# A hybrid SSD, attention and PEER block on one core: the attention's query chunks in pairs over three engines

## The reference, cut to what matters

```python
xn = rmsnorm(h, norm1_g)
z, xbc, dt_raw, q, k, v = split(xn @ w_in)
xbc = silu(causal_depthwise_conv(xbc, conv_w, conv_b))
dt = softplus(dt_raw + dt_bias)
y_ssd = rmsnorm_by_group(ssd_scan(xs, bs, cs, dt, a_log, d_skip) * silu(z), ssd_norm_g)
y_att = rmsnorm(swa_sink_attention(q, k, v, sinks), attn_norm_g)
h = h + concatenate([y_ssd, y_att]) @ w_out
h = h + peer_ffn(rmsnorm(h, norm2_g), wq, keys, u_tab, v_tab)
return rmsnorm(h, norm_f_g)
```

## Time and profile before

| | |
|---|---|
| median of 3 runs | 1706.69 us (1706.01 to 1706.77) |
| the profiled execution | 1707.13 us |
| its span, first to last instruction | 1705.4 us |
| mean granted TensorE clock | 0.998 |
| busy share of the span | PE 99%, DVE 79%, ACT 55%, POOL 33% |

### The profile page before, as it was taken

How to read it: one execution, slowest core, us unless ns; L and a number is a source line. 1 busy time by engine, 2 the same in 40 slices (tenths; PEclk the granted TensorE clock), 3 DMA queues, 4 the chain that set the end, 5 groups by cost and what they waited for, 6 DMA issues and landing times.

```text
span 1705.4 us, 26529 instructions
## 1 busy us (share of the span) xinstructions
PE 1693.4 (99%) x9481; PEld 1472.6 (86%) x9481; DVE 1343.7 (79%) x2129; ACT 930.9 (55%) x1605; POOL 569.1 (33%) x358
## 2 busy tenths in 40 slices
PE   9999999999999999999999999999999999999997
PEld 8889998988888888888888888888888888888886
DVE  7998888878999998554554666668888888888887
ACT  7556755544455554554454454455555555555556
POOL 0120000000017788777783000058555422222210
PEclk9999999999999999999999999999999999999999
DMA  7665568786668887777787888899999999999995
GB/s 272 199 225 172 178 213 267 237 235 199 206 195 197 196 193 197 194 192 201 194 191 221 261 264 262 268 357 340 375 344 361 356 365 365 358 365 365 359 334 157
DMA packets 187042, 444.70 MB, mean 261 GB/s; under 512 B 59472, under 2 KB 94560, under 8 KB 178400
## 3 DMA queue, kind: packets, MB, share of 16 engines
q1 hardware_dynamic: 146688, 371.89, 65.1%
q0 software_dynamic: 40000, 71.55, 15.7%
q10 hardware_dynamic: 288, 0.53, 0.1%
HBM read 423.27 MB, written 20.05 MB: 260 GB/s over the span
## 4 chain that ended last, share of the span: by engine, by line
PE 94%; DVE 3%; ACT 1%; DMA 1%; issue 0%; POOL 0%; SPq 0%; DVEq 0%; ACTq 0%
PE ps L1984 23%; PE ps L2430 20%; PE ps L1990 12%; PE ps L1970 7%; PE ps L2419 7%; PE ps L2421 7%; PE ps L1968 4%; PE ps L2000 3%; PE ps L2319 2%; PE ps L2003 2%; PE ps L2235 1%; PE ps L2322 1%; PE ps L2236 1%; PE ps L2237 1%; DVE low L1088 1%; DMA raw<-v_tab 1%
## 5 line engine op out<-in xcount | busy, mean ns | idle before, releaser
L1088 DVE TENSOR_TENSOR low<-raw,high 128x1024 fp32r<-128x1024 f32 x376 | 458.2, 1224 | 66.3 <-ACT high L705 56.5
L705 ACT ACTIVATE high<-raw 128x1024 fp32r<-128x1024 f32 x376 | 393.1, 1051 | 38.5 <-PE ps L2003 18.9
L1984 PE MATMUL ps<-acts,high 128*128 128x512 f32 x1472 | 350.5, 390 | 0.0
L1984 PEld LDWEIGHTS ps<-acts,high 128*128 128x128 f32 x1472 | 272.7, 188 | 54.1
L656 POOL DMA_INDIRECT big<-v_tab,half_sb x64 | 121.0, 1890 | 465.0 <-DVE big L1856 278.1
L698 ACT ACTIVATE high<-raw 128x1024 fp32r<-128x1024 f32 x172 | 182.6, 1062 | 164.5 <-PE ps L2430 162.4
L1095 DVE TENSOR_TENSOR low<-raw,high 128x1024 fp32r<-128x1024 f32 x172 | 206.2, 1223 | 58.4 <-ACT high L698 58.0
L636 POOL DMA_INDIRECT gate_scratch<-gates_sb,cells_sb x128 | 215.3, 1682 | 69.8 <-issue 69.8
L982 ACT ACTIVATE side<-ps 128x256 f32<-128x256 f32 x128 | 49.1, 383 | 316.2 <-PE ps L1990 213.3
L1990 PEld LDWEIGHTS ps<-acts,low 128*128 128x128 f32 x1472 | 188.8, 191 | 7.2
L1990 PE MATMUL ps<-acts,low 128*128 128x256 f32 x1472 | 191.0, 283 | 0.0
(11 more groups left out here) (311 smaller groups left out, 2925.1 us busy)
## 6 DMA issues: line engine op xcount, KB each, us to landing
raw<-u_tab SPq DMA_DIRECT2D x256, 512.0 KB, 4.4
raw<-v_tab SPq DMA_DIRECT2D x172, 512.0 KB, 7.3
raw_more<-v_tab SPq DMA_DIRECT2D x84, 512.0 KB, 7.5
raw<-w_in SPq DMA_DIRECT2D x60, 512.0 KB, 4.7
raw<-w_out SPq DMA_DIRECT2D x32, 512.0 KB, 5.1
raw<-w_q SPq DMA_DIRECT2D x32, 512.0 KB, 5.2
gate_scratch<-side SPq DMA_DIRECT2D x32, 384.0 KB, 5.7
big<-gate_scratch SPq DMA_DIRECT2D x16, 768.0 KB, 7.1
```

The lines of the kernel that those rows point to most:

```text
L705: nc.scalar.activation(slot(high, s), slot(raw, s), ACT.Copy).then_inc(hi_done, 1)
L1088: V.tensor_tensor(slot(low, s), slot(raw, s), slot(high, s).bitcast(F32), ALU.subtract).then_inc(lo_done, 1)
L1984: mm(both, tile_of(high, kk), both_of(kk), start=(kk == 0), stop=False, skip_group_check=True)
```

## The change

Four edits.

1. `IN_SPLIT` grows by chunks 2 and 3 and by the eight query chunks. So chunks 2 and 3 and all query chunks are projected in pairs (`product_pairs`, `half_pairs`), ACT copies, DVE adds instead of `take`, POOL multiplies.
2. The exponential of the time steps moves from the end of the step c = 5 on ACT, ahead of the first silu, into the step c = 6, ahead of the first tap.
3. `out_pairs` does all sixteen 512-wide matmuls of a chunk and then all sixteen 256-wide ones, instead of eight and eight for each half of the inputs. It waits for `high` first and for `low` later, and both halves' `used` come at the end of their 256-wide matmuls.
4. POOL's list gets the additional multiplies: chunks 2 and 3 first, the query chunks after z.

```diff
-IN_SPLIT = (4, 5, 6, 7, 8, 9) + tuple(range(C_Z, C_Z + SSD_TILES))
+IN_SPLIT = tuple(range(2, 10)) + tuple(range(C_Z, C_Q + SSD_TILES))
...
+            if c >= C_Q:
+                return view(QZ + (c - C_Q) * T, T)
...
-            for c in range(4, 10):
+            for c in range(2, 10):
                 normalise(c)
...
-            for c in range(C_Z + 4, C_Q):
+            for c in range(C_Z + 4, C_OUT):
                 normalise(c)
...
+            copy_low(2)
             for c in range(4, C_Z):
                 cut_high_piece(c + 1, (c + 1) % 2, 0)
+                if c == 6:
+                    act.wait_ge(dt_neg, 1)
+                    nc.scalar.activation(dtv[2], dtv[1], ACT.Exp).then_inc(dt_exp, 1)
                 for k in convs(c):
                     first_tap(k)
                 if c - 1 in IN_SPLIT:
                     copy_low(c - 1)
                 cut_high_piece(c + 1, (c + 1) % 2, 1)
-                if c == 5:
-                    act.wait_ge(dt_neg, 1)
-                    nc.scalar.activation(dtv[2], dtv[1], ACT.Exp).then_inc(dt_exp, 1)
                 for k in convs(c - 1):
                     silu(k)
...
                 if s:
                     exps(s - 1)
+                copy_low(c - 1)
...
-                take(c - 1, (c - 1) % 2, view(QZ + s * T, T), rstd1)
+                add_low(c - 1)
...
-            product(2, 0)
-            product(3, 1)
+            product_pairs(2)
+            product_pairs(3)
...
-            product(C_Q, C_Q % 2)
+            product_pairs(C_Q)
...
-                part(c, 0, every, acc, normed, True, False).then_inc(used, 1)
+                half_pairs(c, 0, True, False).then_inc(used, 1)
...
-                part(c, 1, every, acc, normed, False, True).then_inc(used, 1)
+                half_pairs(c, 1, False, True).then_inc(used, 1)
...
-                for half in range(2):
-                    pe.wait_ge(lo_done, 2 * c + half + 1)
-                    part_pairs(c, half, pair_bank(m) + half).then_inc(used, 1)
+                bank, at = pair_bank(m), 2 * (c % 2) * PIECE
+                for kk in range(KT):
+                    if kk % 8 == 0:
+                        pe.wait_ge(hi_done, 2 * c + kk // 8 + 1)
+                    wh = high[:, at + kk * P:at + (kk + 1) * P]
+                    mm(ps[:, bank + kk // 8, :], wh, act2_both(kk), start=kk % 8 == 0, stop=False, skip_group_check=True)
+                for kk in range(KT):
+                    if kk % 8 == 0:
+                        pe.wait_ge(lo_done, 2 * c + kk // 8 + 1)
+                    wl = low[:, at + kk * P:at + (kk + 1) * P]
+                    ins = mm(ps[:, bank + kk // 8, 0:T], wl, plain(act2_hi)(kk), start=False, stop=kk % 8 == 7,
+                             skip_group_check=True)
+                    if kk % 8 == 7:
+                        ins.then_inc(used, 1)
```

More of the change, by code:

```diff
@@ L2253, in spread @@
                 ins.then_inc(rows_ok, 1)
-            product(C_Q, C_Q % 2)
+            product_pairs(C_Q)
             pe.wait_ge(y_out, SSD_HEADS)
-            normed, mixed = (hi_tile, lo_tile), (plain(act2_hi), plain(act2_lo))
+            mixed = (plain(act2_hi), plain(act2_lo))
             every = range(8)
@@ L2260, in _ @@
                 c = C_Q + 1 + s
-                acc = ps[:, c % 2, 0:T]
                 pe.wait_ge(taken, c - 1)
                 pe.wait_ge(lo_done, 2 * c + 1)
-                part(c, 0, every, acc, normed, True, False).then_inc(used, 1)
+                half_pairs(c, 0, True, False).then_inc(used, 1)
                 if s:
@@ L2312, in _ @@
             part(c1, 1, range(7, 8), att_acc[1], mixed, False, True).then_inc(used, 2)
-            def part_pairs(c, half, bank):
-                s = 2 * (c % 2) + half
-                for k in range(8):
-                    wh = high[:, s * PIECE + k * P:s * PIECE + (k + 1) * P]
-                    mm(ps[:, bank, :], wh, act2_both(8 * half + k), start=(k == 0), stop=False, skip_group_check=True)
-                for k in range(8):
-                    wl = low[:, s * PIECE + k * P:s * PIECE + (k + 1) * P]
-                    ins = mm(ps[:, bank, 0:T], wl, plain(act2_hi)(8 * half + k), start=False, stop=(k == 7),
-                             skip_group_check=True)
-                return ins
             def out_pairs(m):
```

## The result

The changed kernel takes **1712.19 us** (median of 8 runs, 1711.29 to 1713.06), beside 1706.34 for the kernel before on the same chip (8 runs, 1706.01 to 1707.06): ratio 1.0033, 95% interval 1.0024 to 1.0042. The medians are 5.85 us apart, the changed kernel the slower. The profiled execution took 1712.57 us with a span of 1710.9; before, the span was 1705.4.

What follows compares the result with a forecast made beforehand. TensorE's back-to-back matmuls (94% of the span) bound the kernel; early +0.35, attention +6.1 and output -0.2 gave +6.2 us, so 1712.9 us. Forecast case 1708.5 to 1715.5 (chance 0.62), overall range 1705.5 to 1716.5.

Steps and rivals of the forecast that it cites:

- Bound and method: Whole kernel: TensorE's matmuls, 94% of the span, bound it; time taken off PE or spent waiting counts in full.
- The attention, +6.1: Attention's eight logits steps: POOL's multiply waits for DVE's cut (1.65 us), logits come late, PE waits; +6.1 us.
- Rival A: Attention: POOL isn't held up, its multiply takes 0.75 us; +0.3 us in all, 1707.0 us; chance 0.18.
- B: Attention and early part: PE never waits, all pairing is kept; -2.6 us, 1704.1 us; chance 0.07.
- C: Attention steps 1, 6, 7 and chunk 5: POOL passed over again by a second two-input DVE instruction; +4.3, 1717; chance 0.13.
- The early part, +0.35 forecast: Chunks 2 to 8: POOL's multiplies delay DVE 0.8 us before chunk 6, the moved exponential saves 0.44; about +0.35 us.
- the 0.44: Chunk 7: PE's second early wait, about 0.44 us, removed by moving the exponential one chunk later.
- D: Chunks 5 and 6: two added table loads delay ACT's copies, early part stays late; 0.4 us, no separate chance.
- The output, -0.2: Ten output chunks: ordering matmuls by width saves 0.02 us each, 0.2 us in all.

Runs made afterwards that it cites:

- cut_later: Against the changed kernel: in the attention, DVE's cut behind the add, and the low parts of y, made behind the maxes; 1714.28 us, ratio 1.0046.
- dve_waits: Against the changed kernel: in attention steps other than the third, DVE waits for POOL's multiplied query pair before its next cut; 1710.58 us, ratio 1.0024.
- warm_pool: Against the changed kernel: one extra POOL multiply of zeros ahead of its first useful one; 1711.84 us, ratio 1.0030.

## Why the prediction was right, point by point

**Bound and method.** Right: PE's matmuls stay the chain, and each microsecond of waiting in front of them came out as time. Forecast 1712.9, measured 1712.19; against the kernel before, 6.2 us were forecast and 5.85 measured.

**The attention, +6.1.** Right in mechanism and size. POOL's multiply: 1.65 forecast, 1.63 to 1.64 measured. Late steps: 8.80 and 8.79. Gaps forecast 8.27, 8.49, 8.27, 4 times 8.80; measured 8.26, 8.53, 8.32, 8.80, 8.79, 8.79, 8.79. C grew by 6.14: the first logits come 0.51 us late behind chunk 8 (0.5 forecast), the eight take 6.05 us more (6.0), and the rest is 0.42 shorter (0.4). PE's idle time, said to be some 1.4 us in front of each late logits, is 0.43, 1.30, 1.31 and 0.85. Three independent edits (a wait, a halved cut, another engine for the multiply) each moved it as the theory says. The transposes behind the last logits came 6.69 us on (6.70 forecast).

**Rival A.** It did not come: POOL was held up. Its price for the late steps, 7.9 us, was met where POOL was free of the cut (7.88, twice, in cut_later). Its sum, +0.95 for the attention, was not tested, since no run has POOL free with DVE's order and times left alone: dve_waits makes DVE stand still for 0.84 us a step (+4.3 with 0.73 us multiplies), and cut_later moves the cut, which fits elsewhere only in some of the steps. The Trainium skill, GPSIMD Engine Reference, section 3.1, gave 0.82 us by its ratio; the traces show 0.72 to 0.75 for a multiply with no DVE instruction of two SBUF inputs beside it, and 1.64 with the cut.

**Rivals B and C.** B, no waits, did not come. C, passed over again, did not come in the attention: in the last two steps a second instruction of two SBUF inputs stands behind the first, and there it was DVE that waited for POOL (1.75 us instead of 1.22; in step 1, at 164.72, 1.22 instead of 0.68):

```profile
206.82 1.21 DVE L1092 TENSOR_TENSOR low<-raw,high 128x1024 fp32r<-128x1024 f32 x1
207.95 1.75 DVE L1496 TENSOR_TENSOR act_all<-big,act_all 128x1024 fp32r<-128x1024 f32 x1
```

**The early part, +0.35 forecast, -0.24 measured** (A +0.30, B -0.54). Here the sign was wrong; in the total the 0.6 us between the two don't show, since the stated range is 7 us wide. The step that failed is "I charge DVE 0.54 for the first (it meets a cut) and 0.26 for the second (it meets a shorter tap): 0.8 us on DVE ahead of the add that chunk 6 needs", in its first half. In the changed kernel POOL was passed over at the first cut's end and held up nobody: the two cuts took 2.34 us in all, and POOL ended at 41.50, 0.5 us behind the second.

```profile
38.65 2.34 DVE L1092 TENSOR_TENSOR low<-raw,high 128x1024 fp32r<-128x1024 f32 x2
```

```profile
38.81 2.69 POOL L608 TENSOR_TENSOR big<-big 128x256 f32<-128x256 f32 x1 [38.34 <-DVE big L1213]
```

That is rival C's event, at a place where it did good: the 0.54 were not paid. The 0.26 were. POOL's second multiply follows at once (41.46 to 42.27), and of the three taps that DVE runs beside it the second takes 0.75 us instead of 0.48 and the first 0.52 instead of 0.46. The three, before and after:

```profile
41.31 1.50 DVE L1272 SCALAR_TENSOR_TENSOR big<-big,side 128x256 f32<-128x256 f32 x3
```

```profile
41.25 1.82 DVE L1276 SCALAR_TENSOR_TENSOR big<-big,side 128x256 f32<-128x256 f32 x3
```

These 0.32 us are all of A's 0.30. The exponential's move gave the 0.44 read off between chunks 6 and 7 (now 5.70 apart) and 0.10 more between 7 and 8 (5.59, before 5.69). D did not happen: PE stood idle before neither chunk 7 (52.60) nor chunk 8 (58.19).

**The output, -0.2.** Measured -0.19.

## What to carry to other kernels

Before a small step is given to GpSimd, look at what VectorE runs from that moment on: a 0.73 us multiply became 1.64 because a 1.22 us subtract of two SBUF tensors stood beside it, and on a chain that had 0.5 us of slack each of the late steps became 1.2 us longer, seven times the 0.17 us that a pairing saves. When a link of such a chain is shortened, price the order of the engine that is left behind it as well; four of the twelve kernels here shortened the link as planned and lost much or all of the gain at the next thing that the moved instruction fed or held up. And compare stretches that begin at a common event, since the time at which first weights arrive shifted everything behind it by up to 1.4 us here.

## What the runs showed that was not expected

**Who gets in at an instruction's end is not fixed by the neighbours' kind.** The rule of the Trainium skill, SBUF — State Buffer, section SBUF: two separate sides (whoever starts first keeps the shared ports for the whole instruction), agrees with the attention's 1.64 and with DVE's 1.22 for a half cut. It doesn't tell which of two that wait comes next. The same POOL multiply behind the same instructions, that of the first z chunk at 103 us, took 2.58 us in the change and 0.98 in cut_later, whose code up to there is identical. The change, POOL and DVE:

```profile
103.19 2.58 POOL L608 TENSOR_TENSOR big<-big 128x256 f32<-128x256 f32 x1 [1.22 <-DVE big L1213]
```

```profile
103.02 1.02 DVE L1345 TENSOR_TENSOR big<-big 128x384 f32<-128x384 f32 x2
103.95 2.89 DVE L1092 TENSOR_TENSOR low<-raw,high 128x1024 fp32r<-128x1024 f32 x2
```

and cut_later:

```profile
103.10 0.98 POOL L608 TENSOR_TENSOR big<-big 128x256 f32<-128x256 f32 x1 [1.83 <-DVE big L1213]
```

```profile
102.94 1.55 DVE L1345 TENSOR_TENSOR big<-big 128x384 f32<-128x384 f32 x2
104.41 2.35 DVE L1092 TENSOR_TENSOR low<-raw,high 128x1024 fp32r<-128x1024 f32 x2
```

In the first POOL was passed over at the ends of both multiplies and let in behind the first cut (the second cut is the one that waited: 2.89 for two); in the second it was let in behind the first multiply. The first multiply of the early pairs (at 38.81 us in the change) was passed over in all nine kernels that have them. A long pause of POOL's is ruled out as the cause by warm_pool, and by the multiply at 103 us, which was passed over after 1.22 us of idle time in the change and let in after 1.83 in cut_later. The kind of neighbours is ruled out as the whole cause by the same pair of rows. What does decide it stays open. For a forecast it means that a GpSimd multiply among such neighbours has more than one price: 2.58 or 0.98 us at 103 us, and 2.69 at the two cuts of 38.65, where about 1.6 would have ended behind the first.
